# Recurrent chunks of a hybrid trunk: unmasked level products, a predicated write of each level's blocks, and level steps in halves of two heads

## The reference

```
def step(state, inp):                                  # S_t = S_{t-1} diag(w_t) + (S_{t-1} a_t) b_t^T + v_t k_t^T
    r_t, w_t, k_t, v_t, a_t, b_t = inp
    sa = jnp.einsum('bhvk,bhk->bhv', state, a_t)
    state = state * w_t[:, :, None, :] + sa[..., None] * b_t[:, :, None, :] + v_t[..., None] * k_t[:, :, None, :]
    y = jnp.einsum('bhvk,bhk->bhv', state, r_t)
    return state, y
```

## Time and profile before

| what | us |
|---|---|
| time, median of 3 runs (1960.75 to 1962.98) | 1961.38 |
| the profiled execution | 1954.99 |
| its span in the profile | 1953.2 |
| first chunk work to the last chunk's end, in the span | 194 to 390.4 |

### The profile page before, as it was taken

The page is one execution under the profiler, slowest core; times in us unless marked ns, Lnnn a source line. Parts: engine busy times, 40 slices in busy tenths (PEclk is TensorE's granted clock), DMA queues, the critical chain, the costliest instruction groups (busy, mean ns, idle before and its releaser), DMA issues.

```text
span 1953.2 us, 22161 instructions
## 1 busy us (share of the span) xinstructions
PE 1887.5 (97%) x8302; PEld 953.0 (49%) x8302; DVE 601.7 (31%) x1014; ACT 469.4 (24%) x814; POOL 209.9 (11%) x238
## 2 busy tenths in 40 slices
PE   7999999899999999999999999999999999999997
PEld 4554888745564333333333443587453333333333
DVE  2253676631242232231223102311242322313223
ACT  3354333233331111111112103233331111111113
POOL 2000444202010000000001100031100000000001
PEclk9999998899999999999999999999999999999998
DMA  6210100017048999999996312204069999999992
GB/s 184 86 44 0 44 1 1 1 65 256 5 171 360 423 423 424 424 422 423 424 423 267 110 45 86 87 1 161 15 259 423 423 424 424 423 422 423 423 424 95
DMA packets 88415, 465.79 MB, mean 238 GB/s; under 512 B 22303, under 2 KB 24463, under 8 KB 47402
## 3 DMA queue, kind: packets, MB, share of 16 engines
q1 hardware_dynamic: 77600, 450.98, 57.0%
q0 software_dynamic: 4608, 7.92, 1.1%
q10 hardware_dynamic: 6154, 6.15, 1.0%
HBM read 467.59 MB, written 6.29 MB: 243 GB/s over the span
## 4 chain that ended last, share of the span: by engine, by line
PE 86%; DMA 7%; DVE 4%; issue 1%; ACT 1%; POOL 1%; SPq 0%; POOLq 0%; ACTq 0%; DVEq 0%
PE ps L1031 80%; DMA W<-in_moe_w 7%; PE ps L1670 1%; PE ps L1641 1%; PE ps L1237 1%; DVE XI L1955 1%; PE ps L1174 0%; DVE XJ L1951 0%; PE ps L1604 0%; PE ps L1452 0%; POOL sqo L569 0%; DVE XT L1759 0%; POOL memN L569 0%; PE ps L1044 0%; DVE gsn L2087 0%
## 5 line engine op out<-in xcount | busy, mean ns | idle before, releaser
L1031 PE MATMUL ps<-W,xgT 128*64 128x512 f32 x2048 | 453.1, 594 | 4.7 <-DMA W<-in_moe_w 3.4
L1031 PE MATMUL ps<-HT,W 128*128 128x512 f32 (+2 forms) x896 | 342.4, 541 | 2.3 <-DVE HT L1789 1.5
L1031 PEld LDWEIGHTS ps<-W,xgT 128*64 128x64 f32 x2048 | 144.0, 137 | 284.4 <-issue 274.7
L1031 PEld LDWEIGHTS ps<-HT,W 128*128 128x128 f32 (+1 forms) x896 | 169.6, 191 | 164.7 <-issue 155.4
L2215 DVE TENSOR_TENSOR XT<-ps,XT 128x512 f32<-128x512 f32 x240 | 166.0, 692 | 237.2 <-PE ps L1031 237.2
L1031 PE MATMUL ps<-W,act 128*64 128x512 f32 x1024 | 232.3, 595 | 2.8 <-ACT ysb L991 2.8
L1031 PE MATMUL ps<-spread,ysb 128*128 128x512 f32 x512 | 228.3, 599 | 3.2 <-ACT ysb L991 3.2
L2207 DVE TENSOR_TENSOR act<-ps,sl 128x256 f32<-128x256 f32 x64 | 26.9, 420 | 445.3 <-ACT sl L986 445.3
L1031 PEld LDWEIGHTS ps<-spread,ysb 128*128 128x128 f32 x512 | 94.6, 190 | 136.5 <-issue 136.0
L1031 PEld LDWEIGHTS ps<-W,act 128*64 128x64 f32 x1024 | 70.8, 137 | 136.3 <-issue 136.3
L982 ACT ACTIVATE hs<-ps 128x512 f32<-128x512 f32 x64 | 38.2, 597 | 385.5 <-PE ps L1031 385.5
(11 more groups left out here) (405 smaller groups left out, 1780.7 us busy)
## 6 DMA issues: line engine op xcount, KB each, us to landing
W<-in_moe_w SPq DMA_DIRECT2D x256, 1024.0 KB, 17.3
...
```

The costliest lines, as they stand in the source:

```text
L1031: return te.matmul(o, l, r, start=first, stop=last)
```

## The change

The tile `TL` and its masks go: the U product now takes all of A (the first half of `MA`), and its result is more than the level needs. What the level adds is picked out when V is written: `placed` is a `copy_predicated` on DVE that writes V into the right halves of `XJ`'s blocks only where the level's mask is set, 128 elements a partition for two heads. Each step of a level on DVE (write, turn) is cut into halves of two heads, with semaphores to match: PE's U product waits for each half's turn by itself, and V comes in halves, into banks 2, 6, 4, 5 (`INVERSE_BANK`). At level 5 the new `XI` block is a plain copy, and PE computes 32 instead of 64 columns a head for it; at level 6 (`CORNER`) `XJ`'s corner is a plain copy. `XJ` has two buffers, used by chunks in turn; the identity is put in the next one by ACT at level 5 (for chunk 0 by DVE). `begin_inverse` does all four score masks first and no longer waits for `u_done`; that wait is now in `state_factor`, behind it. The `MK` x `TOK` product moves from level 2 to 3, ACT's `decays` from level 3 to 4, the scans of `cumulate` are split over the ends of levels 1 and 2, all four `weighted_keys` come before level 1, and `bonus` j after level j + 1. `score_beta` waits for r = 0 of level 6 before its first half.

```diff
+CORNER = 6
+IX, IV, IU = 4 * LEVELS, 4 * (LEVELS - 1), 2 * (LEVELS - 1)
...
-BONUS_BANK = (7, 6, 5, 7)
+BONUS_BANK = (7, 3, 7, 3)
+INVERSE_BANK = ((2, 6), (4, 5))
...
-        XJ = [sb(f"XJ{r}", [P, 4, CH], at=S3 + (34 + 8 * r) * KB) for r in range(2)]
-        TL = [sb(f"TL{r}", [P, 4, CH], at=S3 + (36 + 8 * r) * KB) for r in range(2)]
+        XJ = [[sb(f"XJ{r}_{b}", [P, 4, CH], at=S3 + (34 + 8 * r + 2 * b) * KB) for r in range(2)] for b in range(2)]
...
-                def mask_level(c, l):
-                    pool.wait_ge(s["iv_u"], c * (2 * LEVELS - 2) + 2 * (l - 1))
-                    g.tensor_tensor(TL[1][:, :, :], MA[c % 2][:, :, 1, 0, :],
-                                    level[:, l, :].unsqueeze(1).broadcast_to([P, 4, CH]), ALU.mult).then_inc(s["iv_tr"], 1)
...
                     mask_keys(c, 1)
-                    mask_level(c, 2)
                     mask_keys(c, 2)
                     mask_keys(c, 3)
-                    mask_level(c, 3)
...
-                        if l == 2:
+                        if l == 3:
                             act.wait_ge(s["akv_done"], c + 1)
                             sc.activation(AKV[:, :], ps[:, 3, :], ACT.Copy).then_inc(s["akv_in"], 1)
-                        if l == 3 and c + 1 < NCH:
+                        if l == 4 and c + 1 < NCH:
                             decays(c + 1)
+                        if l == 5 and c + 1 < NCH:
+                            for r in range(2):
+                                sc.activation(XJ[(c + 1) % 2][r][:, :, :], ident[:, :].unsqueeze(1).broadcast_to([P, 4, CH]),
+                                              ACT.Copy).then_inc(s["iv_id"], 1)
...
                 def score_beta(c):
                     pe.wait_ge(s["ck_el"], c + 1)
+                    if c:
+                        pe.wait_ge(s["iv_x"], c * IX - 2)
                     score(BT, 1, "ck_mat")
                     if c:
-                        pe.wait_ge(s["iv_x"], c * (2 * LEVELS))
+                        pe.wait_ge(s["iv_x"], c * IX)
                     score(BT, 0, "ck_mat")
...
+                    XN, MA_ = XJ[c % 2], MA[c % 2]
                     for l in range(1, LEVELS):
                         for r in range(2):
-                            k = 2 * (l - 1) + r
-                            pe.wait_ge(s["iv_x"], c * (2 * LEVELS) + (k + 1))
-                            pe.wait_ge(s[("iv_tl", "iv_tr")[r]], c * (LEVELS - 1) + l)
                             if c and l == 1 and r == 1:
                                 pe.wait_ge(s["ck_sd"], c)
                             for j in range(4):
-                                ins = mm(ps[:, r, j * P:j * P + P], TL[r][:, j, :], XI[r][:, j, :])
+                                if j % 2 == 0:
+                                    pe.wait_ge(s["iv_x"], c * IX + 4 * (l - 1) + 2 * r + j // 2 + 1)
+                                ins = mm(ps[:, r, j * P:j * P + P], MA_[:, j, r, 0, :], XI[r][:, j, :])
                             ins.then_inc(s["iv_u"], 1)
...
                         if c == NCH - 1 and l <= 4:
 
                             pe.wait_ge(s["bonus_p"], l)
+                            if l == 3:
+                                pe.wait_ge(s["bonus_in"], 1)
                             if l == 4:
-                                pe.wait_ge(s["bonus_in"], 1)
+                                pe.wait_ge(s["akv_in"], c + 1)
                             mm(ps[:, BONUS_BANK[l - 1], :], pair[:, :], KKt[:, l - 1, :]).then_inc(s["bonus_sum"], 1)
-                        if c == NCH - 1 and l == SQUARE:
-                            pe.wait_ge(s["bonus_in"], 3)
-                        if l == 2:
+                        if l == 3:
 
                             pe.wait_ge(s["ck_kmask"], 4 * c + 4)
+                            if c == NCH - 1:
+                                pe.wait_ge(s["bonus_in"], 2)
...
-                            pe.wait_ge(s["iv_ul"], c * (2 * LEVELS - 2) + (k + 1))
+                            pe.wait_ge(s["iv_ul"], c * IU + 2 * (l - 1) + r + 1)
+                            if l == CORNER:
+                                pe.wait_ge(s["iv_j"], 4 * c + 2 * r + 2)
                             for j in range(4):
                                 if l == SQUARE:
-                                    mm(ps[:, 5 + r, j * HD:j * HD + HD], XJ[r][:, j, :], halves(UL[r][:, j, :], l)[0])
-                                ins = mm(ps[:, (2, 4)[r], j * HD:j * HD + HD], UL[r][:, j, :], halves(XJ[r][:, j, :], l)[1])
-                            ins.then_inc(s["iv_v"], 1)
+                                    mm(ps[:, 5 + r, j * 32:j * 32 + 32], XN[r][:, j, :], UL[r][:, j, 0:32])
+                                half_bank = INVERSE_BANK[r][0 if l == SQUARE else j // 2]
+                                ins = mm(ps[:, half_bank, j * HD:j * HD + HD], UL[r][:, j, :], halves(XN[r][:, j, :], l)[1])
+                                if j % 2:
+                                    ins.then_inc(s["iv_v"], 1)
...
+                def cumulate(t, CS=CS, which=range(4)):
+                    for j in which:
                         ins = ve.tensor_tensor_scan(CS[:, j, :], ones[:, :], SGt[:, j, t], 0.0, ALU.mult, ALU.add)
-                    st.then(ins)
-                    ve.tensor_copy(mid.unsqueeze(2), CS[:, :, CH // 2 - 1:CH // 2]).then_inc(s["ck_scan"], 1)
...
+                mask = level[:, :, :].bitcast(I32)
+
+                def flat(x, h):
+                    return x[:, 2 * h:2 * h + 2, :].rearrange("p j t -> p (j t)")
+
+                def placed(dst, src, l, h):
+
+                    w = 1 << l
+                    out = dst[:, 2 * h:2 * h + 2, :].rearrange("p j (b h w) -> p j b h w", h=2, w=w)[:, :, :, 1, :]
+                    valid = mask[:, l, :].rearrange("p (b h w) -> p b h w", h=2, w=w)[:, :, 1, :]
+                    return ve.copy_predicated(out, bcast(valid.unsqueeze(1), [P, 2, P // (2 * w), w]),
+                                              src.rearrange("p (j b w) -> p j b w", j=2, w=w))
 
                 Sf = Sn[:, :, :, :].rearrange("p j r v -> p j (r v)")
 
                 def begin_inverse(c):
 
+                    for i, (q, r) in enumerate(SCORES):
+                        dve.wait_ge(s["ck_mat"], 4 * c + i + 1)
+                        ve.tensor_tensor(MA[c % 2][:, 2 * q:2 * q + 2, r, :, :].rearrange("p j x t -> p j (x t)"),
+                                         ps[:, 4 + 2 * q + r, :].rearrange("p (j n) -> p j n", j=2),
+                                         bcast(tri[:, :, :].rearrange("p x t -> p (x t)").unsqueeze(1), [P, 2, 2 * CH]),
+                                         ALU.mult).then_inc(s["ck_masked"], 1)
+                    dve.wait_ge(s["ck_masked"], 4 * c + 4)
+                    if c:
+                        dve.wait_ge(s["iv_id"], 2 * c)
+                    else:
+                        for r in range(2):
+                            st.did(ve.tensor_copy(XJ[0][r][:, :, :], bcast(ident[:, :].unsqueeze(1), [P, 4, CH])))
+                        st.settle()
                     for r in range(2):
-                        for q in (1, 0):
-                            dve.wait_ge(s["ck_mat"], 4 * c + SCORES.index((q, r)) + 1)
-                            ve.tensor_tensor(MA[c % 2][:, 2 * q:2 * q + 2, r, :, :].rearrange("p j x t -> p j (x t)"),
-                                             ps[:, 4 + 2 * q + r, :].rearrange("p (j n) -> p j n", j=2),
-                                             bcast(tri[:, :, :].rearrange("p x t -> p (x t)").unsqueeze(1), [P, 2, 2 * CH]),
-                                             ALU.mult).then_inc(s["ck_masked"], 1)
-                        dve.wait_ge(s["ck_masked"], 4 * c + 2 * r + 2)
-                        if c:
-                            dve.wait_ge(s["u_done"], c)
-                        st.then(masked(XJ[r], c, r, 0))
-                        st.then(ve.tensor_tensor(XJ[r][:, :, :], XJ[r][:, :, :], bcast(ident[:, :].unsqueeze(1), [P, 4, CH]), ALU.add))
-                        ve.transpose(flat(XI[r]), flat(XJ[r])).then_inc(s["iv_x"], 1)
-                        masked(TL[r], c, r, 1).then_inc(s[("iv_tl", "iv_tr")[r]], 1)
-                        if c and r == 0:
-                            dve.wait_ge(s["ck_exp"], c + 1)
-                            st.then(ve.tensor_tensor(fp, fc, pc, ALU.mult))
-                            st.then(ve.tensor_tensor(Fm[:, :, :], bcast(pair[:, :].unsqueeze(1), [P, 4, P]),
-                                                     bcast(fp.unsqueeze(2), [P, 4, P]), ALU.mult))
+                        st.then(ve.copy_predicated(XJ[c % 2][r][:, :, :], bcast(mask[:, 0, :].unsqueeze(1), [P, 4, CH]), MA[c % 2][:, :, r, 0, :]))
+                        for h in range(2):
+                            ve.transpose(flat(XI[r], h), flat(XJ[c % 2][r], h)).then_inc(s["iv_x"], 1)
+
+                def state_factor(c):
+                    dve.wait_ge(s["ck_exp"], c + 1)
```

(56 more changed lines are left out.)

25 lines of the change are left out of this document (10 added, 15 removed).

## The result

The time after is 1936.69 us (median of 4 runs, 1933.11 to 1938.89) against 1961.61 before (4 runs, 1960.75 to 1962.98): a ratio of 0.9875, 95% interval 0.986 to 0.989, 24.9 us less. The forecast was 1938.7, 22.7 less.

A forecast was written before the change was run, and what follows sets the result against it. PE, busy 97%, was the bound, so only its chain counts. Savings of 3.5 (opening), 1.0, 2.5, 6.6 and 9.1 (chunks 0 to 3) sum to 22.7, from 1961.38 to 1938.7 us; range 1935 to 1948.

The forecast's parts named there:

- The other two signs: Wrong if PE idles over 1 us anywhere in the chunks, or if the clock row there is under 1.00.
- The delay by POOL at level 1: POOL's mask work slows DVE's decay column and scans after level 1: 0.2 us added in chunk 0, 0.6 in 1 and 2.
- The price of the operation: Level step on DVE: predicated write of 128 elements 0.28 us (bounds 0.20 to 0.39), turn of 256 elements 0.445.
- DVE late between chunks: DVE waits for u_done and everything behind slides; after the change all of the late 1.91 us goes.
- The 4.1 of chunk 2: Part of chunk 2's 6.6 us saving, from the lower clock that came behind PE's idle time.
- The 9.1: Chunk 3, U1 to closing products: 40.94 us falls to 31.8, estimated from the same stretch in chunk 1.
- B: Rival, chance 0.16: small DVE instructions cost more, 0.39 us a write, 7.0 in 16 level steps, about 1.0 in opening: 1946.7.
- C: Rival, chance 0.12: lower clock stays once or twice in the chunks, or POOL delays DVE at level 1 fully: 1943 to 1947.
- D: Rival, chance 0.04: no gain, given back later, as where a transfer sets a later stage's end: 1961.
- E: Rival, chance 0.08: slower, predicated write several times the price; break-even 0.35 us more each; at 1.0 us a write, 1984.
- PE's own work, 3.9: Per level, PE's 32 instructions at 0.11 us plus about 0.4 of starts; under the 4.05 ring, which decides.
- The lower bound of the range: 1935 us: writes at 0.20 leave PE's own 3.9 as bound (2.4 less), and no delay by POOL (1.4).

The follow-up runs named there:

- The run with the masks later: Kernel after with POOL's key masks held back until the end of level 1, beside level 2: 1940.42 us, ratio 0.9889.
- masks first: Kernel before with one edit, begin_inverse making all four score masks before it touches XJ: 1954.56 us, ratio 0.9967.
- two runs: Kernel before with four score masks first, u_done wait kept: 1954.56 us; kernel after with the u_done wait put back before the XJ writes: 1936.37 us.
- the run with 3 us of delay: Kernel after with four dummy DVE turns of 512 elements before level 1's first write in chunks 1, 2 and 3: 1948.74 us, ratio 0.9937.

## Why the prediction was right, step by step

**The parts of the sum.** With the prediction's own cuts: V1 of chunk 0 came at 204.41, forecast 204.3, 3.4 saved (3.5). From there to U1 of chunk 1, 1.2 saved (1.0). Chunk 1 41.84, forecast 42.4: 3.05 saved (2.5). Chunk 2 41.82, forecast 42.4: 7.2 saved (6.6). From U1 of chunk 3 to its closing products at 359.12 it took 31.2, forecast 31.8: 9.7 saved (9.1). In all 24.6, forecast 22.7; the last three terms are each 0.6 too small.

**Luck in the total and in the opening.** For the profiled execution 1932.3 was forecast and 1933.11 measured: the stage saved 1.9 more than forecast, and 2.7 was given back behind it, which the prediction had put at nothing. The median was then set 6.4 above the profiled execution, as before; after, it lies 3.6 above. So a total within 2 us of the forecast is in part errors that cancel. In the opening, the second write of 512 took 1.45 beside POOL where 0.69 was forecast, a contention that the prediction had in the chunks and not here; against it the two identity copies took 0.76 together instead of 1.10, and the whole stage began 0.31 earlier in this execution (194.64 against 194.95).

**A sign of being wrong that did come.** "Wrong if a write is over 0.4": the 16 writes of level 1 took 0.40 to 0.45. The other two signs did not come; PE's longest idle in the chunks' stage is the 0.96 of the opening, and the clock is 1.00.

**Where the 0.6 came from.** Two terms were mis-sized and nearly cancel. The delay by POOL at level 1 (0.6 in chunks 1 and 2) was zero: without its `TL` mask POOL was done with the key masks before the decay column and the two scans began at 250.12, and these took 0.13 and 0.74. The run with the masks later shows that the mechanism is real (2.88 for two scans) and only missed its moment. Against it, a write of level 1 costs 0.40 to 0.45, not 0.28, and its period is 4.6 (V1 at 246.18, V2 at 250.80). Beside a chunk without lateness before (chunk 0), the chunk after (chunk 1) stands so: V1 to V2 4.62 against 4.40 (less the 1.73 of `MK` x `TOK`, which before lies here); V2 to V3 3.95 (less the same 1.73) against 4.37; V3 to V4 4.00 against 4.32; V4 to V5 3.98 against 4.31; V5 to U6 3.52 in both; U6 to V6 1.84 against 2.14; the rest equal. So levels 2 to 4 gave 1.07 where 0.81 was forecast, and level 6 gave 0.30 where 0.1 was; level 1 lost 0.22, where a gain of 0.27 less POOL's delay of 0.6 was forecast. That is the 0.6.

**The price of the operation.** The row of a product of that shape, 0.28, was the right neighbour for all levels but the first: all 80 writes of the kernel after, by duration (ns, min/median/max), are

```profile
L1897 DVE COPY_PREDICATED XJ<-level,ps x80: 254/297/448, 205.0 to 356.0; 128x128 f32<-128x128 int32 x80
L1961 DVE STREAM_TRANSPOSE XI<-XJ x64: 445/445/447, 205.5 to 350.4; 128x256 f32<-128x256 f32 x64
```

The turn of 256 was 0.445 to the nanosecond, by the slope of the adds. The estimate of 0.26 from the Trainium skill's formula (VectorE: DVE Perf Modes, "The TRN2 errata — SBUF-src ops pay a fixed extra latency per instruction") meets the writes that follow a turn. Its advice for tiles of 512 or more did not decide: the whole steps were 3.8 us slower by the medians.

**DVE late between chunks.** Right, and shown: masks first heals chunks 1 and 2. The prediction read `u_done` as what everything slides behind; two runs show that this wait was never the cause by itself. It was the row of work behind it: with the masks done earlier, the wait still there, DVE is in time.

**The clock.** The 4.1 of chunk 2 was counted as a consequence of idle time, and the run with 3 us of delay shows that such idle time does bring the clock down, and that this costs 0.8 to 3.3 us besides the idle time itself. The 4.1 itself was not made again by any run; that it came back with the idle time gone is shown by the masks first.

**The last chunk.** The 9.1 was taken from a comparison with chunk 1 and was right in size. The wait that the prediction named, the weighted keys in front of the first bonus product, is in the trace of the kernel before, and a second one beside it (timeline, chunk 3):

```profile
347.94 1.10 PE L1031 MATMUL ps<-KKt,pair 128*128 128x512 f32 x2 [3.13 <-DVE KKt L1912]
...
351.73 0.68 DVE L1885 TENSOR_TENSOR TL<-MA,level 128x512 f32<-128x512 f32 x1
...
353.55 3.78 PE L1031 MATMUL ps<-XI,TL 128*128 128x128 f32 x16 [1.45 <-DVE XI L1955]
```

PE idles 3.13 for the keys, and then 1.45 before U2, behind the level 1 step, which stands in line behind the last keys and the `TL` mask; this the prediction did not name. By the windows from U1 (47.63 to 37.98) PE's idle time falls by 5.7 and its busy time by 4.0 for the same work, at a clock of 0.89 before and 1.00 after; the prediction gave no share to the clock here. In the kernel with the masks first the keys no longer hold up the bonus product, but the same queue stops PE before U2, and moving two keys behind it gave 3.4; in the kernel after the same move gives nothing.

**Where the 24.3 us of the stage come from,** by these runs' windows (195.51 to 171.24): masks first alone 5.7 (1.4, 5.4 and 2.5 in chunks 1 to 3, less the 3.65 lost in the opening and chunk 0); then the unmasked products, the writes and the other moves 12.1 (6.2 in the opening and chunk 0, 5.7 in chunk 3, 0.3 in chunks 1 and 2 together); then the halves 6.5. Of the 24.3 in all, 9.9 are busy time of PE, so mostly the clock, and 14.4 its idle time; the 6.2 of the opening and chunk 0 contain the 2.4 that the lower clock had cost in the kernel with the masks first. By the medians the three steps are 7.9, 14.1 and 3.8. The middle share was not split further: that in the opening it is the two SBUF-to-SBUF masks ahead of each U product is read from the timeline, not tried by itself.

**The rivals.** B (writes at 0.39 throughout) did not come; only level 1 was like it. C did not come in the kernel after; a small edit brought it about in some executions. D did not come beyond the 2.7 us in one pair of executions. E needed 0.35 a write more; the writes of level 1 cost some 0.15 more, the others nothing.

**A term that held for one order only.** "PE's own work, 3.9" was called a floor of the level. It was the cost of 32 instructions with the starts that come of issuing all U, then all V; interleaved they take 3.6. The lower bound of the range rested on that.
